# Conditioning units of 1024 columns, and a head's mean directly behind the split

## The chip, the cores and the metric

The kernel runs on one core of a Trainium2 chip. The metric is the time of one execution on the device in microseconds (us); lower is better. The names of the engines are those of the profile: PE is the matrix engine, DVE the vector engine, ACT the scalar engine, SP the engine that only issues transfers; GpSimd does nothing here.

## The reference

One sequence of 256 positions with 2048 features goes through two blocks, all in float32. Each sublayer is a norm, a modulation by vectors that come from a condition, a mixer, and a gated addition to `x`:

```
mod = silu(c) @ w_ada + b_ada              # 2048 -> 6*2048: sh1 sc1 ga1 sh2 sc2 ga2
h = rms_norm(x, g_norm1) * (1 + sc1) + sh1
qa, ka, va, oa, gates, qb, kb, vb = split(h @ w_in)
h_a = mlstm_bidirectional(qa, ka, va, gates)   # 4 heads of 256
h_a = h_a * rsqrt(mean(h_a**2) + eps) * g_head * sigmoid(oa)
h_b = neighborhood_attention(qb, kb, vb)       # 8 heads of 128
x = x + ga1 * (concat(h_a, h_b) @ w_out)
h = rms_norm(x, g_norm2) * (1 + sc2) + sh2
x = x + ga2 * conv_glu(h, w_up, w_down)
x = rms_norm(x, g_final)
# second block: the same frame twice, shift, scale, gate = silu(c2) @ ada_w + ada_b,
# once with a spatial gating unit (sgu), once with latent attention (mla)
```

The twelve modulation vectors need a product of one row with a matrix of 2048 x 24576: 201 MB of weights that are read for a single row.

## The kernel before

**Matrices.** Every large weight comes in pieces of 1 MB (the `w_down` pieces are smaller) through four slots `raw`. For each piece ACT writes the high part `w_hi`, rounded to float32r (`split`, L1105), DVE the low part `w_lo = raw - w_hi` over the slot of `raw` (`split`, L1557), and PE multiplies high by high, high by low and low by high (L575 and L576 for stages in columns, L614 to L616 for stages in tokens). The pieces have one order for the whole kernel (`STAGES`): `ka qa va qb kb vb oa` (together `w_in`, 8 pieces each), `w_out`, `w_up0`, `w_down0`, `w_up1`, `w_down1`, the `sgu` stages, `lat`, `mla_z`, `mla_v`, `heads`, `mla_out`. ACT and DVE are two pieces ahead of PE (`AHEAD`); SP issues the load of piece q when PE has done piece q - 4, and ACT may split piece q when PE has done piece q - 3 (there are three `w_hi`).

**Order on an engine.** Every engine runs its own list in order. For each piece ("slot") DVE first does `begin`: the split of the piece two ahead, then a possible urgent step, then the conditioning pieces that are put on this slot. After that it adds the second half of the product (`second_half`, L1611) and does what the slot has of attention. ACT's `begin` is the split and then the loads of conditioning pieces, each of which waits until DVE has used the buffer; then follow squares or exponents, the copy of the first half (L1124), roots.

**Conditioning.** The shift and scale of the first norm (the first 64 of 384 pieces of 512 KB) are made at the start by DVE and PE together (`first_piece`, L1622, on 128x1024). The other 320 pieces are DVE's alone (`add_ada`): a unit is 512 output columns, and a piece holds two of the 16 chunks of 128 input features for them. DVE adds each chunk, times silu(c), to `acc` (128x512): the second add waits for the first, `chain.link`. The last piece of a unit has an end: a transpose in 32x32 blocks (L1576) and a sum over 32 (L1577) to `fold`, from which PE makes the columns of `mods` with a few small matmuls (`fold_group`). `ADA_SPANS` says on which slots the pieces stand: (stage, first slot, slots, pieces), spread evenly. Four buffers `ada` hold them; ACT loads the piece four further on as soon as one is used.

**Heads of the mLSTM.** `A_STEPS` puts the steps of head k on slots: scores, mix, norm. After the mix DVE has `hf` (L1762, L1765); on the next slot (`A_SQUARES`: `qb` 2, `qb` 7, `kb` 4, `vb` 1) ACT takes the squares (L1202), DVE the mean (`a_head_mean`, L1771), ACT the root (L1207); on the slot behind it DVE starts with `a_head_diagonal` (L1775, L1777), PE multiplies by that diagonal after its own piece (L790), and DVE takes the result (L1783). Behind the heads come ten waves of neighbourhood attention, one per slot from `vb` 3 (`B_WAVES`): PE scores (L824), DVE arguments and maximum (L1805 to L1809), ACT exponents (L1230), on the next slot DVE's scaling as its urgent step (`b_scale`, L1792, L1794), PE transposes (L802), and so on. At the end of `w_in` the mixers' outputs are gated and split (`mix_high`, `gated` L1814, `mix_low` L1818) while PE begins `w_out`.

Of the kernel before, what the change touches and what calls it, by code (L numbers as in the profile page):

```python
# [76 lines left out]
for _name in STAGES:  # L77
# [6 lines left out]
    else:  # L84
# [8 lines left out]
SH1, SC1, GA1, SH2, SC2, GA2, S0, C0, G0, S1, C1, G1 = range(12)  # L93
UNITS = 4
UCOLS = D // UNITS
APIECES = 8
APIECE = D // P // APIECES * UCOLS
FIRST_UNITS = 2 * UNITS
QUARTERS = 4
FIRST_PIECES = QUARTERS * KC  # L100
K_PE = [3, 6, 9, 12]
# [3 lines left out]
FIRST_USED = QUARTERS * len(K_DVE)  # L105
ADA_SPANS = [("ka", 5, 11, 18), ("va", 0, 8, 15), ("qb", 0, 16, 28), ("vb", 0, 15, 19), ("w_out", 0, 13, 16),
             ("w_up0", 0, 40, 32), ("w_down0", 0, 32, 24), ("w_up1", 0, 44, 24), ("w_down1", 0, 26, 16), ("sgu_v", 3, 29, 40),
             ("sgu_u", 0, 32, 24), ("sgu_z", 0, 32, 24), ("sgu_out", 0, 28, 24), ("lat", 0, 20, 16)]
ADA_AT, _p = {}, FIRST_UNITS * APIECES
for _s, _j, _slots, _n in ADA_SPANS:  # L110
# [54 lines left out]
def build(nc, a):  # L165

    with ExitStack() as ctx:
# [49 lines left out]
        e1 = work("e1", [P, ASLOTS, APIECE], 0)  # L217
        acc_first = work("acc_first", [P, 2, 2 * UCOLS], 13312)
        row = work("row", [P, 2 * UCOLS], 15360)
        gw_lo = work("gw_lo", [P, GPAD], 4096, F32R)  # L220
# [16 lines left out]
        decay = work("decay", [P, 2, 2 * T], 13312)  # L237
        neg_rows = work("neg_rows", [P, 2 * T], 14336)
        bias_b = work("bias_b", [P, NH_B * 6, GRID_W], 14848)
        diag_a = at_("diag_a", [P, TT, P], o_nt)  # L240
# [32 lines left out]
        diag = work("diag", [P, TT, P], 2560)  # L273
        cst = work("cst", [P, 1152], 16384)
        turn, mask_m, cos, sin = cst[:, 0:256], cst[:, 256:640], cst[0:ROPE, 0:256], cst[0:ROPE, 640:896]
        rot, twice = cst[0:ROPE, 896:1024], cst[0:ROPE, 1024:1152]
        kr1 = work("kr1", [P, T], 13312)[0:ROPE, :]
        kro = work("kro", [P, T], 12288)
# [259 lines left out]
        def _(pe):  # L538
            def fold_group(n):


                v, count = FOLDS[n]
                if n == 0:
                    pe.wait_ge(sel_in, 16)
                    pe.wait_ge(unit_taken, FIRST_UNITS)
# [77 lines left out]
            def row_piece(q, k):  # L623

                p = q * KC + k
                if k == K_PE[0] and q:
                    pe.wait_ge(row_copied, 2 * q)
                pe.wait_ge(ada_full[p % 8], (p // 8 + 1) * 16)
                for v in range(2):
                    mm = pe.matmul(px[1 + v][0:1, :], csil[:, 0, k:k + 1], first_buf(p)[:, v * UCOLS:(v + 1) * UCOLS],  # L630
                                   start=(k == K_PE[0]), stop=(k == K_PE[-1]))
                mm.then_inc(ada_rowed, 1)
# [198 lines left out]
            def w_in_after(part, j):  # L831
                if (part, j) == ("ka", 7):
                    pe.wait_ge(rows_ready, 1)
                    for sc in range(TT):
                        pe.transpose(px[1][:, sc * GROW:(sc + 1) * GROW], gates[0:GROW, 5, sc * P:(sc + 1) * P],
                                     ident[0:GROW, 0:GROW])
                        mm = pe.transpose(px[1][:, (TT + sc) * GROW:(TT + sc + 1) * GROW], neg_rows[0:GROW, T + sc * P:T + (sc + 1) * P],
                                          ident[0:GROW, 0:GROW])
# [257 lines left out]
        def _(act):  # L1096
# [141 lines left out]
            for part, j in W_IN_PIECES:  # L1238
# [308 lines left out]
        def _(dve):  # L1547
# [166 lines left out]
            def gate_step(n):  # L1714
# [14 lines left out]
                elif n == 2:  # L1729
# [91 lines left out]
            for part, j in W_IN_PIECES:  # L1821
# [236 lines left out]
            for c in range(MH):  # L2058
# [90 lines left out]
def constants():  # L2149
# [53 lines left out]
def lay_out(i):  # L2203
# [107 lines left out]
```

## Time and profile before

| | |
|---|---|
| median of 3 runs | 2464.03 us (2463.12, 2464.03, 2468.52) |
| the profiled execution's own time | 2468.54 us |
| its span, first to last instruction | 2466.4 us |
| mean granted PE clock | 0.986 |
| busy: PE, DVE, ACT | 97%, 79%, 45% |
| instructions | 31962 |

Busy time is the time in which at least one instruction of the engine runs; PE's matmuls overlap, so its 97% does not say that it runs at its peak. A wait is named by the engine and instruction that ended it. The granted clock is PE's, as a share of 2.4 GHz.

### The profile page before, as it was taken

The page shows a single profiled execution, that of the slowest core. Times are in us where ns is not written, and L with a number is a line of the kernel's source. Part 1 is how long each engine was busy: PE and PEld are TensorE (multiplying, and loading weights), DVE is VectorE, ACT ScalarE, POOL GpSimd, SP SyncE. Part 2 cuts the span into 40 slices and gives each one's busy share as a digit, 9 for nine tenths or more (in the row PEclk, how much of TensorE's full clock was granted, in tenths as well). Part 3 has the DMA queues.
Part 4 walks back from the last instruction along what each step waited for, and adds up shares of the span by engine and source line. Part 5 has one row for each costly group of instructions (what it writes and reads, how often), then busy time and mean ns, then how long its engine had stood idle before and what let it go on. Part 6 is the DMA issues. An engine that isn't in the chain of part 4 may idle for free.

```text
span 2466.4 us, 31962 instructions
## 1 busy us (share of the span) xinstructions
PE 2402.6 (97%) x12970; PEld 2043.8 (83%) x12970; DVE 1947.9 (79%) x2412; ACT 1112.8 (45%) x1381; POOL 0.2 (0%) x4
## 2 busy tenths in 40 slices
PE   6999999998999999999998999999999998999999
PEld 3587888887888888888887888888888887888987
DVE  6789988898888788877787889778787666774754
ACT  2143444545444434444444444644445334555642
POOL 0000000000000000000000000000000000000000
PEclk8799999999999999999999999999999999999999
DMA  9799777585767688666685899766777774654343
GB/s 396 291 363 343 271 259 258 210 309 195 258 252 258 230 294 296 239 236 238 225 269 186 307 327 320 261 237 223 256 265 254 273 265 164 248 205 158 118 169 137
DMA packets 119011, 620.33 MB, mean 252 GB/s; under 512 B 13392, under 2 KB 14672, under 8 KB 76112
## 3 DMA queue, kind: packets, MB, share of 16 engines
q1 hardware_dynamic: 70560, 446.45, 51.1%
q10 hardware_dynamic: 48304, 171.82, 18.9%
q8 instruction: 103, 1.69, 0.3%
q14 instruction: 44, 0.36, 0.0%
HBM read 616.13 MB, written 2.10 MB: 251 GB/s over the span
## 4 chain that ended last, share of the span: by engine, by line
PE 77%; DVE 16%; DMA 3%; ACT 3%; issue 1%; ACTq 0%; SPq 0%; DVEq 0%
PE pm L575 21%; PE pm L576 11%; PE ps L575 10%; DVE w_lo L1557 7%; PE ps L576 5%; DVE acc L1570 5%; PE pm L614 5%; PE pm L616 5%; PE pm L615 5%; ACT w_hi L1105 2%; PE ps L614 2%; PE ps L616 2%; PE ps L615 2%; DMA ada<-in_ada 2%; PE px L894 1%
## 5 line engine op out<-in xcount | busy, mean ns | idle before, releaser
L1557 DVE TENSOR_TENSOR w_lo<-raw,w_hi 128x2048 fp32r<-128x2048 f32 (+2 forms) x412 | 891.8, 2165 | 312.7 <-ACT w_hi L1105 311.0
L1105 ACT ACTIVATE w_hi<-raw 128x2048 fp32r<-128x2048 f32 (+2 forms) x412 | 746.8, 1813 | 465.9 <-DMA raw<-in_w_down 124.9
L575 PE MATMUL pm<-h,w_hi 128*128 128x512 f32 x2318 | 826.3, 400 | 3.5 <-DVE w_lo L1557 3.0
L576 PE MATMUL pm<-h,w_lo 128*128 128x256 f32 x2318 | 651.0, 281 | 0.0
L575 PEld LDWEIGHTS pm<-h,w_hi 128*128 128x128 f32 x2318 | 436.4, 188 | 113.1 <-issue 7.6
L1570 DVE SCALAR_TENSOR_TENSOR acc<-ada,csil,acc 128x512 f32<-128x512 f32 x600 | 449.4, 749 | 12.7
L576 PEld LDWEIGHTS pm<-h,w_lo 128*128 128x128 f32 x2318 | 438.6, 189 | 0.2
L575 PE MATMUL ps<-h,w_hi 128*128 128x512 f32 x1186 | 422.9, 399 | 0.8 <-DVE w_lo L1557 0.8
L576 PE MATMUL ps<-h,w_lo 128*128 128x256 f32 x1186 | 332.8, 281 | 0.0
L575 PEld LDWEIGHTS ps<-h,w_hi 128*128 128x128 f32 x1186 | 222.7, 188 | 56.6 <-issue 2.7
L576 PEld LDWEIGHTS ps<-h,w_lo 128*128 128x128 f32 x1186 | 224.0, 189 | 0.1
L575 PE MATMUL pm<-glu,w_hi 128*128 128x512 f32 x484 | 170.0, 395 | 0.0
L614 PE MATMUL pm<-w_hi,h 128*128 128x512 f32 x352 | 139.0, 395 | 5.5 <-DVE h L1676 5.0
L615 PE MATMUL pm<-w_lo,h 128*128 128x512 f32 x352 | 137.8, 392 | 0.0
L616 PE MATMUL pm<-w_hi,h 128*128 128x512 f32 x352 | 137.8, 391 | 0.0
L576 PE MATMUL pm<-glu,w_lo 128*128 128x256 f32 x484 | 135.9, 281 | 0.0
L575 PEld LDWEIGHTS pm<-glu,w_hi 128*128 128x128 f32 x484 | 90.9, 188 | 21.4
L576 PEld LDWEIGHTS pm<-glu,w_lo 128*128 128x128 f32 x484 | 91.1, 188 | 0.0
L1342 ACT ACTIVATE conv<-conv 128x256 f32<-128x256 f32 x44 | 18.4, 418 | 157.9 <-DVE conv L1898 157.9
L614 PEld LDWEIGHTS pm<-w_hi,h 128*128 128x128 f32 x352 | 66.6, 189 | 19.9 <-issue 5.4
L616 PEld LDWEIGHTS pm<-w_hi,h 128*128 128x128 f32 x352 | 66.6, 189 | 14.1
L615 PEld LDWEIGHTS pm<-w_lo,h 128*128 128x128 f32 x352 | 66.7, 189 | 13.6
(430 smaller groups left out, 3034.8 us busy)
## 6 DMA issues: line engine op xcount, KB each, us to landing
ada<-in_ada ACTq DMA_DIRECT2D x320, 512.0 KB, 5.3
raw<-in_w_up SPq DMA_DIRECT2D x88, 1024.0 KB, 4.9
raw<-in_w_in SPq DMA_DIRECT2D x56, 1024.0 KB, 6.0
raw<-in_w_down SPq DMA_DIRECT2D x64, 704.0 KB, 5.2
raw<-in_sgu_v SPq DMA_DIRECT2D x32, 1024.0 KB, 5.1
raw<-in_sgu_u SPq DMA_DIRECT2D x32, 1024.0 KB, 5.0
raw<-in_sgu_z SPq DMA_DIRECT2D x32, 1024.0 KB, 4.9
raw<-in_sgu_out SPq DMA_DIRECT2D x32, 1024.0 KB, 5.0
```

What stands on the lines that cost most here:

```text
L575: pe.matmul(dst[:, :], wh[:, k, :], hl, start=(kc == 0), stop=False, skip_group_check=True)
L576: mm = pe.matmul(dst[:, 0:T], wl[:, k, :], hi, start=False, stop=last, skip_group_check=True)
L614: pe.matmul(dst[:, :], h_hi, wh[:, k, :], start=(kc == 0), stop=False, skip_group_check=True)
L615: pe.matmul(dst[:, :], h_hi, wl[:, k, :], start=False, stop=False, skip_group_check=True)
L616: mm = pe.matmul(dst[:, :], h_lo, wh[:, k, :], start=False, stop=(kc == 4 * parts - 1), skip_group_check=True)
L894: mm = pe.matmul(px[g % 4][:, c * T + n * P:c * T + (n + 1) * P], v_sgu[:, n, g * 2 * P + c * P:g * 2 * P + (c + 1) * P], mixw[s][:, r, 0: ...
L1105: act.activation(w_hi[:, q % HSLOTS, 0:n], raw[:, q % SLOTS, 0:n], ACT.Copy).then_inc(hi_ready, 1)
L1342: act.activation(conv[:, k % 2, :], conv[:, k % 2, :], ACT.Gelu).then_inc(gelu_ready, 1)
L1557: tt_(w_lo[:, q % SLOTS, 0:n], raw[:, q % SLOTS, 0:n], whole(w_hi[:, q % HSLOTS, 0:n]), ALU.subtract).then_inc(lo_ready, 1)
L1570: ins = stt(dst, w, c, dst, ALU.mult, ALU.add)
```

## The change

The change has two parts that speak of time and some moves of buffers.

- `UNITS` 4 becomes 2 and `APIECES` 8 becomes 16: a unit is 1024 columns, a piece (still 128 partitions of 1024 elements, 512 KB) holds one chunk of 128 input features for them. `add_ada` does one operation on 128x1024 per piece instead of two on 128x512; transpose and sum at the end of a unit are over 128x1024. There are still 320 pieces behind the start; the start itself keeps its widths (`QCOLS` takes the place of `UCOLS` there).
- `ADA_SPANS`: `ka` from slot 4 (17 pieces over 12 slots; before 18 over 11 from slot 5), `va` 13 (15), `qb` and `kb` 27 (28), `vb` and `oa` 20 over 14 slots (19 over 15), `w_out` 19 (16). From `w_up0` on nothing moves.
- `a_head_mean` becomes the urgent step of `begin` on its slots: behind the split, ahead of the conditioning pieces and of `second_half`, where it stood at the end of the slot.
- `acc` grows by 2 KB per partition. Room for it comes from: the second half of `neg_rows` goes to `gates[:, 7]`, the first into `nt`; `bias_b` moves by 512 columns; `cst` loses 128 columns, for which the doubled rotary key is read from partitions 64 to 127.

```diff
-UNITS = 4
+UNITS = 2
 UCOLS = D // UNITS
-APIECES = 8
+APIECES = 16
...
+QCOLS = D // QUARTERS
...
-ADA_SPANS = [("ka", 5, 11, 18), ("va", 0, 8, 15), ("qb", 0, 16, 28), ("vb", 0, 15, 19), ("w_out", 0, 13, 16),
+ADA_SPANS = [("ka", 4, 12, 17), ("va", 0, 8, 13), ("qb", 0, 16, 27), ("vb", 0, 14, 20), ("w_out", 0, 13, 19),
...
-FOLD_UNITS = 12
+FOLD_UNITS = 6
...
-        neg_rows = work("neg_rows", [P, 2 * T], 14336)
-        bias_b = work("bias_b", [P, NH_B * 6, GRID_W], 14848)
+        neg_rows = at_("neg_rows", [P, T], o_nt + T)
+        bias_b = work("bias_b", [P, NH_B * 6, GRID_W], 14336)
...
-        cst = work("cst", [P, 1152], 16384)
+        cst = work("cst", [P, 1024], 16384)
...
                 dve.wait_ge(ada_full[p % ASLOTS], p // ASLOTS * 16 + 16 - FIRST_PIECES // 8 * 16)
-                for r in range(2):
-                    w, c = ada[:, p % ASLOTS, r * UCOLS:(r + 1) * UCOLS], csil[:, cond, 2 * k + r:2 * k + r + 1]
-                    if k + r == 0:
-                        ins = ts_(dst, w, c, None, ALU.mult)
-                    else:
-                        ins = stt(dst, w, c, dst, ALU.mult, ALU.add)
-                    if r == 0:
-                        chain.link(ins)
+                w, c = ada[:, p % ASLOTS, :], csil[:, cond, k:k + 1]
+                if k == 0:
+                    ins = ts_(dst, w, c, None, ALU.mult)
+                else:
+                    ins = stt(dst, w, c, dst, ALU.mult, ALU.add)
                 if k == APIECES - 1:
                     chain.link(ins)
-                    turned = ada[:, p % ASLOTS, 0:UCOLS]
+                    turned = ada[:, p % ASLOTS, :]
...
-                    stt(neg_rows[G, T:2 * T], gates[G, 4, :], -1.0, gates[G, 6, :], ALU.mult, ALU.subtract).then_inc(rows_ready, 1)
+                    stt(gates[G, 7, :], gates[G, 4, :], -1.0, gates[G, 6, :], ALU.mult, ALU.subtract).then_inc(rows_ready, 1)
...
-                begin(part, j, (lambda: b_scale(w - 1)) if 0 < w <= NH_B else None, part != "ka" or j >= 2)
+                urgent = (lambda: b_scale(w - 1)) if 0 < w <= NH_B else None
+                if (part, j) in A_SQUARES:
+                    urgent = lambda: a_head_mean(A_SQUARES[part, j])
+                begin(part, j, urgent, part != "ka" or j >= 2)
...
-                if (part, j) in A_SQUARES:
-                    a_head_mean(A_SQUARES[part, j])
...
-                    tt_(kr1, kr1, krt, ALU.add).then_inc(kr_ready, 1)
+                    tt_(kr_sum, kr1, krt, ALU.add).then_inc(kr_ready, 1)
```

## Rows read from the trace of the kernel before

**Rows 1.** Busy time, share of the span and instructions of each engine
```profile
PE 2402.6 (97%) x12970; PEld 2043.8 (83%) x12970; DVE 1947.9 (79%) x2412; ACT 1112.8 (45%) x1381; POOL 0.2 (0%) x4
```
**Rows 2.** PE's waits: 120:250, 250:400, 400:470, 470:500, 600:835 (us, times, longest)
```profile
PE pm L575 <- DVE w_lo L1557: 2.3, 2, 1.7
PE pm L614 <- ACT va L1271: 0.5, 1, 0.5
...
PE px L790 <- DVE diag_a L1777: 4.1, 2, 3.1
...
PE px L802 <- DVE s_b L1794: 1.0, 1, 1.0
...
PE pm L575 <- DVE h L1818: 2.2, 1, 2.2
...
PE ps L575 <- DVE w_lo L1557: 0.8, 2, 0.6
PE pm L575 <- DVE w_lo L1557: 0.7, 3, 0.3
```
**Rows 3.** Stretches: us, busy of each engine, PE clock, DMA share, GB/s
```profile
349.80:353.20 3.40, 3.40 (x14) 3.11 (x15) 2.51 (x2) 2.93 (x3) 0.00 (x0) 0.51 0.91 337
...
483.00:486.40 3.40, 3.33 (x10) 2.84 (x11) 3.35 (x7) 3.40 (x5) 0.00 (x0) 0.50 0.17 72
```
**Rows 4.** SP's issues: first start, us to the last one's end, count
```profile
128.63 16.97 SPq L515 DMA_DIRECT2D raw<-in_w_in  x4
...
600.25 212.05 SPq L515 DMA_DIRECT2D raw<-in_w_up  x38
...
963.16 220.81 SPq L515 DMA_DIRECT2D raw<-in_w_up  x40
...
843.11 80.41 SPq L515 DMA_DIRECT2D raw<-in_w_down  x22
...
1210.13 89.73 SPq L515 DMA_DIRECT2D raw<-in_w_down  x24
```
**Rows 5.** DVE's groups, whole span: count, busy us, mean ns, idle before
```profile
L1570 DVE SCALAR_TENSOR_TENSOR acc<-ada,csil,acc 128x512 f32<-128x512 f32 x600 | 449.4, 749 | 12.7
L1622 DVE SCALAR_TENSOR_TENSOR acc_first<-e,csil,acc_first 128x1024 f32<-128x1024 f32 x24 | 30.8, 1284 | 7.3 <-DMA e<-in_ada 5.3 <-DVE acc_first L1622 0.5
L1576 DVE STREAM_TRANSPOSE ada<-acc 128x512 f32<-128x512 f32 x40 | 28.5, 712 | 1.4
L1577 DVE TENSOR_REDUCE fold<-ada 128x16 f32<-128x512 f32 x40 | 27.4, 686 | 1.4
```
**Rows 6.** Timeline of DVE and ACT at head 2: start, us, instruction, idle before
```profile
348.89 0.17 DVE L1775 RECIPROCAL small_a<-small_a 128x2 f32<-128x2 f32 x1 [0.27 <-ACT small_a L1207]
...
350.69 2.29 DVE L1557 TENSOR_TENSOR w_lo<-raw,w_hi 128x2048 fp32r<-128x2048 f32 x1 [1.12 <-ACT w_hi L1105]
...
341.43 0.42 ACT L1202 ACTIVATE sqt<-hf 128x256 f32<-128x256 f32 x1 [4.29 <-DVE hf L1765]
...
348.65 0.20 ACT L1207 ACTIVATE small_a<-small_a 128x2 f32<-128x2 f32 x1 [4.75 <-DVE small_a L1771]
```
**Rows 7.** Timeline of DVE: bias in `qa` 4, half of `oa` 6
```profile
187.24 3.36 DVE L1833 TENSOR_TENSOR bias_b<-bias_b,wmask 128x3072 f32<-128x3072 f32 x1
...
475.85 0.42 DVE L1611 TENSOR_TENSOR oa<-oa,pm 128x256 f32<-128x256 f32 x1
```
**Rows 8.** Timeline of DVE and PE at `vb` 5
```profile
406.00 0.62 DVE L1794 TENSOR_SCALAR s_b<-s_b,small_b 128x256 f32<-128x256 f32 x2
...
407.20 0.60 PE L802 MATMUL px<-ident,s_b 128*128 128x128 f32 x4
```
**Rows 9.** ACT's issues near 130 us, and the bias load's time to landing
```profile
130.04 0.46 ACTq L1251 DMA_DIRECT2D bias_b<-in_bias_b  x1
145.71 0.82 ACTq L1110 DMA_DIRECT2D ada<-in_ada  x2
...
bias_b<-in_bias_b ACTq DMA_DIRECT2D x1, 1536.0 KB, 15.6
```

More of the change, by code:

```diff
@@ L93 @@
 SH1, SC1, GA1, SH2, SC2, GA2, S0, C0, G0, S1, C1, G1 = range(12)
-UNITS = 4
+UNITS = 2
 UCOLS = D // UNITS
-APIECES = 8
+APIECES = 16
 APIECE = D // P // APIECES * UCOLS
-FIRST_UNITS = 2 * UNITS
 QUARTERS = 4
+QCOLS = D // QUARTERS
 FIRST_PIECES = QUARTERS * KC
@@ L105 @@
 FIRST_USED = QUARTERS * len(K_DVE)
-ADA_SPANS = [("ka", 5, 11, 18), ("va", 0, 8, 15), ("qb", 0, 16, 28), ("vb", 0, 15, 19), ("w_out", 0, 13, 16),
+ADA_SPANS = [("ka", 4, 12, 17), ("va", 0, 8, 13), ("qb", 0, 16, 27), ("vb", 0, 14, 20), ("w_out", 0, 13, 19),
              ("w_up0", 0, 40, 32), ("w_down0", 0, 32, 24), ("w_up1", 0, 44, 24), ("w_down1", 0, 26, 16), ("sgu_v", 3, 29, 40),
              ("sgu_u", 0, 32, 24), ("sgu_z", 0, 32, 24), ("sgu_out", 0, 28, 24), ("lat", 0, 20, 16)]
-ADA_AT, _p = {}, FIRST_UNITS * APIECES
+ADA_AT, _p = {}, FIRST_PIECES
 for _s, _j, _slots, _n in ADA_SPANS:
@@ L217, in build @@
         e1 = work("e1", [P, ASLOTS, APIECE], 0)
-        acc_first = work("acc_first", [P, 2, 2 * UCOLS], 13312)
-        row = work("row", [P, 2 * UCOLS], 15360)
+        acc_first = work("acc_first", [P, 2, 2 * QCOLS], 13312)
+        row = work("row", [P, 2 * QCOLS], 15360)
         gw_lo = work("gw_lo", [P, GPAD], 4096, F32R)
@@ L273, in build @@
         diag = work("diag", [P, TT, P], 2560)
-        cst = work("cst", [P, 1152], 16384)
+        cst = work("cst", [P, 1024], 16384)
         turn, mask_m, cos, sin = cst[:, 0:256], cst[:, 256:640], cst[0:ROPE, 0:256], cst[0:ROPE, 640:896]
-        rot, twice = cst[0:ROPE, 896:1024], cst[0:ROPE, 1024:1152]
-        kr1 = work("kr1", [P, T], 13312)[0:ROPE, :]
+        rot, twice = cst[0:ROPE, 896:1024], cst[ROPE:P, 896:1024]
+        kr_both = work("kr_both", [P, T], 13312)
+        kr1, kr_sum = kr_both[0:ROPE, :], kr_both[ROPE:P, :]
         kro = work("kro", [P, T], 12288)
@@ L544, in fold_group @@
                     pe.wait_ge(sel_in, 16)
-                    pe.wait_ge(unit_taken, FIRST_UNITS)
+                    pe.wait_ge(unit_taken, 2 * QUARTERS)
                 else:
@@ L629, in row_piece @@
                 for v in range(2):
-                    mm = pe.matmul(px[1 + v][0:1, :], csil[:, 0, k:k + 1], first_buf(p)[:, v * UCOLS:(v + 1) * UCOLS],
+                    mm = pe.matmul(px[1 + v][0:1, :], csil[:, 0, k:k + 1], first_buf(p)[:, v * QCOLS:(v + 1) * QCOLS],
                                    start=(k == K_PE[0]), stop=(k == K_PE[-1]))
@@ L836, in w_in_after @@
                                      ident[0:GROW, 0:GROW])
-                        mm = pe.transpose(px[1][:, (TT + sc) * GROW:(TT + sc + 1) * GROW], neg_rows[0:GROW, T + sc * P:T + (sc + 1) * P],
+                        mm = pe.transpose(px[1][:, (TT + sc) * GROW:(TT + sc + 1) * GROW], gates[0:GROW, 7, sc * P:(sc + 1) * P],
                                           ident[0:GROW, 0:GROW])
@@ L971, in doubled_key @@
                 pe.wait_ge(kr_ready, 1)
-                pe.matmul(px[1][:, T:2 * T], twice, kr1, start=True, stop=True).then_inc(kr_twice, 1)
+                pe.matmul(px[1][:, T:2 * T], twice, kr_sum, start=True, stop=True).then_inc(kr_twice, 1)
             for c in range(MH):
@@ L1165, in copy_rows @@
                 for v in (1, 0):
-                    act.activation(row[0:1, v * UCOLS:(v + 1) * UCOLS], px[1 + v][0:1, :], ACT.Copy).then_inc(row_copied, 1)
+                    act.activation(row[0:1, v * QCOLS:(v + 1) * QCOLS], px[1 + v][0:1, :], ACT.Copy).then_inc(row_copied, 1)
             def first_chunks(q):
@@ L1246, in _ @@
                     for k in range(ASLOTS):
-                        load_ada(FIRST_UNITS * APIECES + k)
+                        load_ada(FIRST_PIECES + k)
                 if (part, j) == ("ka", 4):
                     act.dma_start(wmask[:, :], a["wmask"]).then_inc(wmask_in, 16)
-                    act.wait_ge(unit_summed, FIRST_UNITS)
+                    act.wait_ge(unit_summed, 2 * QUARTERS)
                     act.dma_start(flat(bias_b[:, :, :]), a["bias_b"]).then_inc(bias_in, 16)
@@ L2162, in constants @@
     win = np.where((c[None] >= lo) & (c[None] < lo + WIN_COLS), 0.0, NEG).astype(f)
-    cst = np.zeros((P, 1152), f)
+    cst = np.zeros((P, 1024), f)
     half = ROPE // 2
@@ L2177, in constants @@
     for m in range(P):
-        cst[m % ROPE, 1024 + m] = 1.0
+        cst[ROPE + m % ROPE, 896 + m] = 1.0
     sel = np.zeros((P, 2 * P - BLOCK), f)
@@ L2268, in lay_out @@
     ada = np.concatenate([i["w_ada"][0], i["ada_w_2"][0], i["ada_w_2"][1]], axis=1)
-    first = ada[:, 0:2 * D].reshape(KC, P, 2, QUARTERS, UCOLS).transpose(3, 0, 1, 2, 4).reshape(-1, P, APIECE)
+    first = ada[:, 0:2 * D].reshape(KC, P, 2, QUARTERS, QCOLS).transpose(3, 0, 1, 2, 4).reshape(-1, P, APIECE)
     ada = ada.reshape(APIECES, KC // APIECES, P, 12 * UNITS, UCOLS).transpose(3, 0, 2, 1, 4)
```

## The prediction

> **What bounds the kernel now.** The page comes first: TensorE (PE) is busy 97% of the span [rows 1], so whatever VectorE (DVE) saves counts only where PE waits for DVE. The waits of PE say where that is [rows 2]. Behind the start, which the change leaves alone, and outside the norms, whose waits hang on squares, sums and roots that no conditioning piece stands ahead of, they are: 2.3 us on `w_lo` and 0.5 us on the copy of `va` between 120 and 250 us; 4.1 us on `diag_a` (heads 0 and 2, the longest 3.1) between 250 and 400; 1.0 us on `s_b`; 2.2 us on `h` at the end of `w_in`; and 0.8 + 0.7 us on `w_lo` in `w_up0`. That is 11.6 us. Two of them cost more than they last: behind the 3.1 us wait and behind the 2.2 us wait the granted clock is 0.51 and 0.50 for 3.4 us (the 1.2 GHz level) [rows 3], 1.7 us of PE's work each, while the 1.7 us wait among those on `w_lo` is followed by no such row.
>
> The third view is the queue of weight loads, because one `raw` load is issued as each piece ends on PE. In `w_up0` 38 issues start over 212 us, (212.05 - 0.33) / 37 = 5.72 us a piece; in `w_up1`, the same matmuls, 40 over 220.8, 5.65 us [rows 4]. So `w_up0` loses 37 x 0.07 = 2.6 us, more than its 1.5 us of visible waits. But PE has also two paces of its own: four issues in `ka` stand 5.55 us apart, and those in `w_up1`, where no wait on DVE is seen, 5.65 [rows 4]. I return to that below. From `w_up1` on PE waits for DVE nowhere except at the norms and once each for a residual and a head.
>
> **The change part by part.** (1) *Piece adds.* 320 pieces behind the first norm. Now a piece is two adds of 128x512, 0.749 us each; then it is one of 128x1024, and that very form stands in the start: 1.284 us [rows 5]. Per piece 2 x 0.749 - 1.284 = 0.21 us, and a step between dependent adds of 0.03 us less: 0.25 us. The first piece of a unit is a plain multiply, cheaper in both; it changes the sum little.
> (2) *Unit ends.* 40 become 20. One costs 0.712 + 0.686 us now [rows 5]. For twice the columns the bounds are 1.40 us (nothing saved) and half of the fixed part less; with the slope of the adds, (1.284 - 0.749) / 512 = 1.04 ns a column, it is 1.24 + 1.22 = 2.46 us. I take 2.5. Sum over the kernel: 300 x 0.25 + 20 x (2.8 - 2.5) + first pieces, some 85 us of DVE time; nearly all of it lies where PE is at its own pace and buys nothing.
> The Trainium skill ("VectorE: DVE Perf Modes", the section on the TRN2 errata) says that operations on SBUF pay a fixed latency once per instruction, and gives (N + 151) / 0.96 ns for a float32 add. By that a merged pair would save 0.16 us instead of 0.21; the row decides, and either frees more than the waits need.
>
> (3) *Slots.* Counting the spans out: through `qa` 7 DVE has 6.5 us less of this work, through `va` 7 15 us, through `kb` 4 22 us. The ends of units fall on `qa` 6, `qb` 0, `kb` 2, `vb` 4 and `w_out` 1 instead of `qa` 1, `qa` 6, `va` 2, `va` 6, `qb` 3, `kb` 0, `kb` 4, `vb` 1, `vb` 7 and `oa` 6. Each new one is a lump: piece and end are 3.8 us, now 2.9.
>
> (4) *The mean.* Today it stands behind the adds and the second half. At head 2 ACT's root waits for it until 348.65, 4.75 us idle, and ACT takes up its next split only then, so that DVE stands 0.27 us before the reciprocal and 1.12 us before `w_lo` [rows 6]. Directly behind the split DVE finds ACT's squares done (two of 0.42 us [rows 6] under a split of 2.3 us, so the wait on `a_sq` is covered; uncovered it would be about 1.2 us for each of four heads, with the adds behind it). The root, the next split and `diag_a` no longer wait for the adds: 0.16 + 0.27 + 1.12, about 1.5 us of DVE time per head.
>
> (5) `neg_rows`, `kr_sum` and `cst` change places, not sizes (cst is 64 KB smaller, its load is hidden): nothing.
>
> Now the waits, one after another.
> *120 to 250 us:* the `w_lo` wait of 1.7 us follows the 3.4 us bias addition in `qa` 4 [rows 7]. The 6 us less of adds before it cover the 1.7. The `va` copy waits in ACT behind loads that wait for DVE's adds; that goes too. Gain 2.8 to 3.0 us; I take 3.0.
> *Head 0 and head 2:* from the point where DVE waits for PE's scores of head 2 in `kb` 1 I add up: split 2.3, adds 4.6 (`kb` 2, now 3.1), half 0.4, split 2.3, adds 2.6 (`kb` 3, now 1.5), half 0.4, then the mix at about 337, 2 us ahead of today; `kb` 4 has one piece (1.3) where two and an end stand today (4.5 us). `diag_a` is there at about 344.4, and PE asks for it at 346.6. Gain 4.1 us and the slow stretch of 1.7: 5.8 (bounds 1.0, head 0 alone, and 5.8).
> *`s_b`:* `vb` 7 has 2.0 us less ahead of it: 1.0 us.
> *End of `w_in`:* `oa` 6 loses its piece and unit end, 2.9 us, but its half cannot be added before PE and ACT deliver it, near 474.4 against 475.85 [rows 7]; from there the chain of `hx`, gate and `h` is as long as before. So only some 1.1 us of the first wait go, and 0.4 us come back at the next four chunks: 0.7 us. The rest is too short for a slow stretch, by the 1.7 us wait that had none: 1.7 more. Gain 2.4 (bounds 0.7 and 3.9).
> *`w_up0`:* the loop split, adds, `glu`, half, split, adds, taps, gelu, split paces it; per ten pieces the adds fall from 13.9 to 10.3 or 12.4 us, enough for PE's pace: 2.6 us (bounds 1.5 and 2.6).
> *A new wait:* `vb` 4 gets 4.6 us of adds where it has 1.5. Behind them stand the arguments of wave 1, ACT's exponents, and after the next split the scaling, at 406.00, for which PE asks at 407.20 [rows 8]. DVE reaches `vb` 4 about 1 us earlier; it is through 3.1 - 1.0 = 2.1 us later than now, and the scaling, 0.62 us and the reciprocal's step, ends at 408.8 to 409.0 against 407.2: a loss of 1.8 us (bounds 0 and 3.5, the latter with a slow stretch).
> *The start at `ka` 4:* two ACT loads are issued near 140 instead of 145.71 us [rows 9], while the raw load for `qa` 0 is under way; `w_lo` has under 1 us to spare there. Bounds 0 and 2 us. The bias load, issued at 130.04, is in flight for 15.6 us [rows 9] on the same ACT queue, up to about 146, so the new loads stand behind it: I take 0.
> The Trainium skill ("DMA: Bandwidth & Descriptors", Queues, rings and completion order) says that each DMA engine takes turns between the queue rows that have work, packet by packet. By that, SP's load keeps its turn as long as ACT's row has work anyway, which it has here; it speaks against the early start only where ACT's queue is empty.
>
> **Sum:** 3.0 + 5.8 + 1.0 + 2.4 + 2.6 - 1.8 - 0 = 13.0 us. The profiled execution took 2468.5 us (span 2466.4), so its like would take 2455.5. The median of the runs is 2464.0, 4.5 us less. The two paces explain such a step (44 pieces of `w_up1` x 0.1 = 4.4), though no row shows it. I carry the 13.0 over: **2451.0 us**.
>
> **Rivals.** *Part of it only* (2459): the heads and the end of `w_in` are held by PE and ACT, not by DVE; then 3.0 + 1.0 + 2.6 - 1.8 = 4.8 us go. For it: the head's chain has six hand-overs. Against: DVE is idle under 0.5 us at a time there, except for the 1.12. *The lumps bite more* (2455): the `vb` 4 wait brings a slow stretch, and another comes at `qb` 0 or `kb` 2. *Early loads* (2453, or 2455 with a slow stretch): the loads pulled to 140 us take bandwidth from the raw load, and PE waits up to 2 us for `qa` 0. *Pace, upward:* pieces at 5.65 us fall to 5.55; of `w_up1` alone 4.4 us, 2446; all 160 such pieces 16 us, 2435. *Pace, downward, the slower case:* PE's own pace turns from fast to slow in stretches that this change does not touch, since the end of a wait sets it anew. `w_down0` stands at 3.81 us and `w_down1` at 3.89 [rows 4]: 32 x 0.07 = 2.4 us; `w_up1` of the median run 4.4. The kernel becomes slower than before by 0.2% only from 18 us on, 1.9% of some 950 us of matmuls that now run fast. No row speaks for so many at once.
>
> **Numbers.** The forecast with all its terms 0.60 (its own range 2446 to 2456); part only 0.14; lumps 0.08; early loads 0.03; pace upward 0.09; pace downward 0.06, of which 0.03 ends slower. Range 2443 to 2460: up to the partial case above, and to `w_up1` and one more stage at the fast pace below. Within 0.2%, 4.9 us, a measurement can't tell from no change: faster means below 2459.1. Partial cases split there, so faster 0.84, same 0.12, slower 0.04.
>
> **What would show it.** Adds of 128x1024 at 1.28 us, 300 of them, unit ends near 2.5 us; no wait on `diag_a`, or one under 0.5 us; no `w_lo` wait between 150 and 250; a wait of 1 to 2 us on `s_b` near 400 us, in another wave than now; one of 1 to 1.5 us at the start of `w_out`, no stretch of 0.5 clock from 120 us to the second norm; `w_up0` at 5.65 us a piece; every stage from `w_down0` on as long as before but for steps of 0.1 us per piece. Wrong would be: `diag_a` still waited for (ACT is late, not DVE), `w_lo` waits in `w_up0` at the unit ends (`w_up0` 18 and 38), or a new wait at `qa` 0.

## The result and the profile after

The changed kernel takes 2452.38 us (median of 5 runs, 2449.22 to 2455.29); the kernel before, on the same chip, 2465.75 (5 runs, 2463.12 to 2468.52). The ratio is 0.9944 with an interval of 0.9933 to 0.9955: 13.4 us or 0.56% faster. The forecast was 2451.0 (2443 to 2460), 13.0 us less than a median of 2464.0. The profiled execution took 2449.22 us, its span is 2447.3 us, the mean granted clock 0.990.

The page's row of busy time, which answers to [rows 1]:

```profile
PE 2390.6 (98%) x12970; PEld 2037.4 (83%) x12970; DVE 1873.4 (77%) x2052; ACT 1115.4 (46%) x1381; POOL 0.2 (0%) x4
```

DVE is busy 74.5 us less, and the time fell by a fifth of that: DVE did not bound the kernel, it only made PE wait in places. The groups of DVE that answer to [rows 5]:

```profile
L1570 DVE SCALAR_TENSOR_TENSOR acc<-ada,csil,acc 128x1024 f32<-128x1024 f32 x300 | 383.9, 1280 | 1.5
L1574 DVE STREAM_TRANSPOSE ada<-acc 128x1024 f32<-128x1024 f32 x20 | 24.9, 1245 | 0.7
L1575 DVE TENSOR_REDUCE fold<-ada 128x32 f32<-128x1024 f32 x20 | 24.4, 1220 | 0.7
L1568 DVE TENSOR_SCALAR acc<-ada,csil 128x1024 f32<-128x1024 f32 x20 | 15.0, 748 | 0.1
```

An add of 128x1024 takes 1.280 us, as the start's form did. A unit end is 2.47 us (1.245 + 1.220) where 2.5 was reckoned. The last number of a row, idle time before the group, fell from 12.7 to 1.5 us for the adds: the waits between the two dependent halves are gone.

PE's waits, in the same stretches as [rows 2] (the work stands 7 to 17 us earlier). Between 120 and 250 us there is none. Between 250 and 400, and between 400 and 470, one each:

```profile
PE px L803 <- DVE s_b L1792: 1.7, 1, 1.7
...
PE pm L576 <- DVE h L1816: 0.8, 1, 0.8
```

Of the 11.6 us of waits the 0.8 on `h` are left, and 0.3 on `w_lo` at the beginning of `w_up0`. The 1.7 us on `s_b` are new: they stand in another wave than the 1.0 did. The granted clock of the whole stretch, which holds no half-clock part as [rows 3] had (columns as there):

```profile
120.00:560.00 440.00, 434.21 (x2359) 373.18 (x2358) 382.61 (x408) 204.91 (x235) 0.00 (x0) 1.00 0.81 291
```

The new wait comes from what stands in DVE's timeline around `vb` 4 (start, us, instruction):

```profile
382.07 0.62 DVE L1792 TENSOR_SCALAR s_b<-s_b,small_b 128x256 f32<-128x256 f32 x2
382.60 1.28 DVE L1570 SCALAR_TENSOR_TENSOR acc<-ada,csil,acc 128x1024 f32<-128x1024 f32 x1
383.91 1.25 DVE L1574 STREAM_TRANSPOSE ada<-acc 128x1024 f32<-128x1024 f32 x1
385.19 1.22 DVE L1575 TENSOR_REDUCE fold<-ada 128x32 f32<-128x1024 f32 x1
386.44 0.75 DVE L1568 TENSOR_SCALAR acc<-ada,csil 128x1024 f32<-128x1024 f32 x1
387.23 0.76 DVE L1803 SCALAR_TENSOR_TENSOR s_b<-px,bias_b 128x256 f32<-128x256 f32 x2
...
391.22 0.62 DVE L1792 TENSOR_SCALAR s_b<-s_b,small_b 128x256 f32<-128x256 f32 x2
```

The end of the unit and the first piece of the next, 4.6 us together, stand ahead of the arguments of the wave (387.23), so its scaling is done at 391.8, and PE's transposes start then, 1.7 us late.

**Stage by stage.** For each piece the trace has the moment at which PE reports it done, and the table takes differences of those (us). "start" runs to the end of `ka` 3 (the first half of `ka`), which the change does not touch; "rest" is everything behind `w_up1` up to the last piece of `mla_out`. All kernels that ran stand in it, since the executions of one kernel lie 5 to 18 us apart. A single stage repeats within a few tenths where nothing waits and the pace is the same; the two traces of the kernel before differ by some 1.5 us in `qb`, `kb` and in `vb`, by 2.7 in `w_down0` and by 4.6 in `w_up1`.

| kernel | start | ka | qa, va | qb, kb | vb | oa | w_out | w_up0 | w_down0 | w_up1 | rest | without start |
|---|---|---|---|---|---|---|---|---|---|---|---|---|
| before | 128.6 | 22.2 | 93.2 | 122.6 | 53.9 | 59.0 | 93.4 | 261.7 | 122.9 | 248.7 | 1247.1 | 2324.8 |
| e11 before again | 124.0 | 22.5 | 93.1 | 121.1 | 55.5 | 59.0 | 93.6 | 262.3 | 125.6 | 244.1 | 1244.6 | 2321.4 |
| after | 121.9 | 22.6 | 88.5 | 116.5 | 55.7 | 57.8 | 90.9 | 260.0 | 123.5 | 248.9 | 1248.0 | 2312.4 |
| e8 after again | 121.4 | 22.7 | 88.5 | 116.5 | 55.7 | 57.6 | 91.0 | 260.0 | 122.9 | 248.7 | 1246.8 | 2310.5 |
| e1 mean back | 121.4 | 22.2 | 89.4 | 116.5 | 55.7 | 57.7 | 91.0 | 259.5 | 122.9 | 248.7 | 1249.6 | 2313.2 |
| e2 mean only | 125.3 | 22.6 | 92.5 | 117.6 | 53.8 | 59.0 | 93.5 | 261.8 | 125.3 | 244.1 | 1247.0 | 2317.2 |
| e3 old spans | 121.5 | 23.2 | 89.4 | 116.5 | 53.8 | 57.8 | 94.1 | 259.9 | 123.2 | 244.4 | 1248.1 | 2310.4 |
| e4 two halves | 121.4 | 23.9 | 88.5 | 116.5 | 55.9 | 57.7 | 91.0 | 259.9 | 123.2 | 248.7 | 1247.3 | 2312.7 |
| e9 halves waited | 128.3 | 22.6 | 89.2 | 117.0 | 57.9 | 57.8 | 92.9 | 261.1 | 122.9 | 248.7 | 1249.3 | 2319.3 |
| e5 spans only | 123.8 | 22.3 | 90.5 | 117.2 | 57.9 | 58.8 | 92.2 | 261.9 | 122.9 | 248.7 | 1245.4 | 2317.7 |
| e6 end moved | 125.4 | 22.2 | 89.4 | 116.5 | 53.8 | 58.7 | 90.9 | 260.4 | 124.0 | 248.7 | 1249.8 | 2314.3 |
| e10 end alone | 121.6 | 22.2 | 89.3 | 116.5 | 53.8 | 57.7 | 91.0 | 260.6 | 124.1 | 248.7 | 1250.6 | 2314.4 |
| e12 adds alone | 121.6 | 22.6 | 88.5 | 116.5 | 53.8 | 57.7 | 95.5 | 260.4 | 123.4 | 248.7 | 1248.5 | 2315.6 |
| e7 start ka 5 | 122.0 | 23.4 | 88.5 | 116.5 | 55.7 | 57.8 | 91.0 | 259.5 | 122.9 | 248.7 | 1250.3 | 2314.3 |

### The profile page after: what moved, and what is told of

Its sections match the earlier page's. It is cut to its first block, busy times and chain, and to the rows that moved or that the text cites. A ratio compares the mean times of both kernels' runs of the same rounds, so it can differ in the third digit from the quotient of the medians.

```text
span 2447.3 us, 31602 instructions
## 1 busy us (share of the span) xinstructions
PE 2390.6 (98%) x12970; PEld 2037.4 (83%) x12970; DVE 1873.4 (77%) x2052; ACT 1115.4 (46%) x1381; POOL 0.2 (0%) x4
## 4 chain that ended last, share of the span: by engine, by line
PE 80%; DVE 2%; ACT 0%; DMA 0%; issue 0%; ACTq 0%; DVEq 0%
PE pm L576 24%; PE pm L577 12%; PE ps L576 12%; PE ps L577 6%; PE pm L615 4%; PE pm L616 4%; PE pm L617 4%; PE ps L615 2%; PE ps L616 2%; PE ps L617 2%; DVE w_lo L1558 1%; PE px L895 1%; PE pm L594 0%; DVE x L2023 0%; PE ps L594 0%; PE pm L1011 0%
## 5 line engine op out<-in xcount | busy, mean ns | idle before, releaser
L1570 DVE SCALAR_TENSOR_TENSOR acc<-ada,csil,acc 128x1024 f32<-128x1024 f32 x300 | 383.9, 1280 | 1.5
L576 PEld LDWEIGHTS pm<-glu,w_hi 128*128 128x128 f32 x484 | 90.9, 188 | 21.9 <-DVE w_lo L1558 0.4
```

Source lines behind the costliest of these rows:

```text
L576: pe.matmul(dst[:, :], wh[:, k, :], hl, start=(kc == 0), stop=False, skip_group_check=True)
```

## The experiments

The change has three parts that speak of time: the wide units with their merged adds, the new slots, and the early mean. The moves of buffers stand in every variant of the changed kernel, e9 included, and were not tested by themselves. Sums "without the start" are the last column of the table.

### Is it the mean? (e1, e2)

e1 is the changed kernel with the mean back at the end of the slot; e2 is the kernel before with only the mean moved.

```diff
-                urgent = (lambda: b_scale(w - 1)) if 0 < w <= NH_B else None
-                if (part, j) in A_SQUARES:
-                    urgent = lambda: a_head_mean(A_SQUARES[part, j])
-                begin(part, j, urgent, part != "ka" or j >= 2)
+                begin(part, j, (lambda: b_scale(w - 1)) if 0 < w <= NH_B else None, part != "ka" or j >= 2)
...
+                if (part, j) in A_SQUARES:
+                    a_head_mean(A_SQUARES[part, j])
```

> The changed kernel with the mean of a head put back behind the second half of its slot. If the wide adds carry the gain (my theory), DVE reaches the head steps early anyway: the wait on diag_a stays under 0.5 us at every head, each head shows again the idle 1.1 us before w_lo, and the time is that of the changed kernel within 2 us (2451 to 2454). If the moved mean carries the 5.8 us of heads 0 and 2 (rival), a wait of 2 to 3 us on diag_a comes back with a stretch at half the clock, and the time is 2456 to 2458.

> The kernel before with the mean behind the split and nothing else. My theory: diag_a at head 2 comes 1 to 2 us earlier and the 3.1 us wait shrinks to 1.5 to 2 us without the slow stretch, the waits on w_lo, s_b and h at the end of w_in stay; 2459 to 2463. Rival (the mean is the change): all head waits go, 2457. Rival (the mean is nothing): 2465.

e1: 2450.09 us (2446.92 to 2457.46), ratio 0.9952 (0.9936 to 0.9968): as fast as the change. Its `qb` and `kb` take the same 116.5 us, and its waits up to the end of `w_in` are those of the changed kernel. e2: 2457.72 us (2455.01 to 2467.27), 0.9979 (0.9965 to 0.9994), so the mean alone gives some 5 us. I had expected 2459 to 2463; the rival's 2457 is what came, though not all head waits went, as it said. PE's waits of e2 between 120 and 400 us:

```profile
PE pm L575 <- DVE w_lo L1557: 2.0, 2, 1.7
PE px L790 <- DVE diag_a L1777: 0.7, 1, 0.7
PE pm L614 <- ACT va L1271: 0.4, 1, 0.4
PE ps L614 <- DVE qa L1611: 0.2, 1, 0.2
```

The wait on `diag_a` at head 2, 3.1 us before, is gone, where I had expected half of it to stay, and 0.7 of 1.1 us stay at head 0. The waits on `w_lo` (2.0 us, 2.3 before), `va`, `s_b` and `h` are within 0.3 us of [rows 2]. The mean alone cures head 2, and beside the other parts it is worth nothing: that wait was cured more than once.

### Is it the slots? (e3, e5, e7)

e3 is the changed kernel with the old `ADA_SPANS`, e5 the kernel before with the new ones, e7 the changed kernel with `("ka", 5, 11, 17)`, which undoes the early start alone.

```diff
-ADA_SPANS = [("ka", 4, 12, 17), ("va", 0, 8, 13), ("qb", 0, 16, 27), ("vb", 0, 14, 20), ("w_out", 0, 13, 19),
+ADA_SPANS = [("ka", 5, 11, 18), ("va", 0, 8, 15), ("qb", 0, 16, 28), ("vb", 0, 15, 19), ("w_out", 0, 13, 16),
```

> Wide units and the moved mean, but the pieces on the slots of before (18, 15, 28, 19, 16). Ends of units then fall on qa 6, va 6, kb 0, vb 1 and oa 6. My theory: the wait of 1.7 us on s_b at vb 5 goes, since the lump is not on vb 4, and the wait on h at the start of w_out grows from 0.8 to 2 us or more, perhaps with 3.4 us at half the clock, since oa 6 has a piece and an end again; in all within 2 us of the changed kernel. Rival (the spread is what gains): 2457 or more.

> The kernel before, units of 512 columns and the mean where it was, with only the new slots for the pieces (17, 13, 27, 20, 19). My theory: one to two pieces fewer before the waits in qa and va and at head 2, and none on oa 6: 1 to 4 us faster than before, 2461 to 2464. Rival (the spread is the gain): 2455 or less.

> The changed kernel with the first conditioning piece on ka 5 as before (17 pieces over 11 slots). My theory (the early loads stand behind the bias load): within 1 us of the changed kernel. Rival (early loads take bandwidth from the raw load of qa 0): the piece of qa 0 or the one before is 0.2 to 2 us shorter than in the changed kernel.

e3: 2452.93 us (2444.97 to 2457.92), ratio 0.9949 (0.9931 to 0.9966). In the table it has 53.8 us in `vb` and 94.1 in `w_out`. The new spans lose 1.9 us in `vb` by their lump and give 3.2 in `w_out`, so 1.3 us net, which the medians here can't tell. What `w_out` had is a wait on `h` as before the change, and slow clock behind it (waits from 460 to 480 us, and a stretch of 3.4 us):

```profile
PE pm L576 <- DVE h L1816: 2.8, 1, 2.8
```
```profile
467.60:471.00 3.40, 3.40 (x13) 2.87 (x13) 3.24 (x7) 2.53 (x3) 0.00 (x0) 0.56 0.00 0
```

e5: 2460.09 us (2454.23 to 2466.91), ratio 0.9996 (0.9982 to 1.0011). Without the cheaper adds the gain of the slots alone can't be told from nothing by the times; the one trace is 3.7 to 7.1 us shorter without the start than the two of the kernel before. It shows them give and take: the wait on `diag_a` falls from 4.1 to 0.2 us, and `s_b` is waited for 4.4 us in three waves, one of them 1.9, which was not expected.

e7: 2450.96 us (2444.30 to 2456.01), ratio 0.9960 (0.9945 to 0.9975). `ka` took 23.4 us against 22.6, `qa` 0 6.12 us in both: the early loads cost nothing, as forecast. The tenths that `ka` varies by (22.2 to 23.9) go with neither start slot.

### Is it the width of the operation? (e4, e9)

Both keep units, ends, slots and mean of the change, and add each piece as two operations on the halves of the unit. In e4 the two don't wait for each other; in e9 the second waits for the first (the two lines marked with +9), so that the adds cost what they cost before.

```diff
-                w, c = ada[:, p % ASLOTS, :], csil[:, cond, k:k + 1]
-                if k == 0:
-                    ins = ts_(dst, w, c, None, ALU.mult)
-                else:
-                    ins = stt(dst, w, c, dst, ALU.mult, ALU.add)
+                c = csil[:, cond, k:k + 1]
+                for r in range(2):
+                    cols = slice(512 * r, 512 * (r + 1))
+                    w, part = ada[:, p % ASLOTS, cols], acc[:, cols]
+                    if k == 0:
+                        ins = ts_(part, w, c, None, ALU.mult)
+                    else:
+                        ins = stt(part, w, c, part, ALU.mult, ALU.add)
+9                    if r == 0:
+9                        chain.link(ins)
```

> The changed kernel, each piece added in two operations of 128x512 on the halves of its 1024 columns, with no wait between them: units, ends, slots and mean are those of the changed kernel, only the merged operation is gone. My theory (DVE's time per piece is what counts): adds cost 1.50 us a piece again, waits on w_lo in qa and in w_up0 and one on diag_a come back, 2459 to 2465. Rival (unit width, slots and mean do it): 2451 to 2453.

> The changed kernel with each piece added as two operations on 128x512 (the halves of the unit) and the second made to wait for the first, so that a piece costs DVE what it did before the change (about 1.53 us against 1.28 with one operation and 1.41 with two that don't wait, as the previous run showed), while slots, mean and unit ends stay those of the change. If DVE time per piece is what the change lives on: the rows between the third piece of ka and the end go back toward the kernel before with the new spans alone: w_lo waits in w_up0 return (w_up0 261.5 to 262 us against 260.0), w_out near 92 against 91, vb 57 to 58 against 55.7 with two s_b waits, about 5 to 6 us longer in all than the changed kernel; kb and qb stay cured by the early mean and the slots. If it is the width of a unit and the place of its ends: all stages as in the changed kernel within 1 us.

e4: 2449.46 us (2445.75 to 2454.21), ratio 0.9940 (0.9919 to 0.9961), as fast as the change. Up to `w_up1` its stages are within 0.3 us of the change's, except `ka` (1.3 longer). My expectation of 2459 to 2465 was wrong: the merged operation as such does not carry the gain, and a piece did not cost the 1.50 us that I had put down. The groups of DVE show why, first of e4, then of e9:

```profile
L1573 DVE SCALAR_TENSOR_TENSOR acc<-ada,csil,acc 128x512 f32<-128x512 f32 x600 | 422.8, 746 | 1.5
```
```profile
L1573 DVE SCALAR_TENSOR_TENSOR acc<-ada,csil,acc 128x512 f32<-128x512 f32 x600 | 449.7, 749 | 12.1
```

600 operations of 746 ns would be 447.6 us one behind the other, and the group is busy 422.8: the two of a piece overlap. With the idle time a piece costs 1.41 us in e4, 1.54 in e9 ((449.7 + 12.1) / 300), 1.28 in the change. Half of the saving is that the operations of a piece no longer depend on each other, half that there is one instead of two.

The Trainium skill ("VectorE: DVE Perf Modes", the section on the TRN2 errata) says that the latency to SBUF is exposed between instructions and that one large tile pays it once. This case agrees in kind: one add in place of two free ones saves 1.41 - 1.28 = 0.13 us, where its formula for the addition of two tensors (151 cycles at 0.96 GHz) gives 0.16. The further 0.13 us that a wait between them costs, measured here, are not in that formula.

e9: 2458.24 us (2456.07 to 2462.51), ratio 0.9978 (0.9969 to 0.9987). Against the change and its second trace, without the start, it is 6.9 to 8.8 us longer; the expectation for costly adds said 5 to 6. 1.7 us of this are a stretch at half clock that the change does not have. In `w_up0` it lost 1.1 us where 1.5 to 2 were expected. Its waits up to the end of `w_in`, and the clock behind the largest:

```profile
PE px L803 <- DVE s_b L1797: 2.2, 1, 2.2
PE pm L576 <- DVE h L1821: 0.8, 1, 0.8
PE pm L576 <- DVE ka L1614: 0.5, 1, 0.5
PE px L791 <- DVE diag_a L1780: 0.4, 1, 0.4
PE ps L615 <- DVE qa L1614: 0.3, 1, 0.3
```
```profile
400.50:403.90 3.40, 3.40 (x11) 2.71 (x9) 0.86 (x2) 2.05 (x3) 0.00 (x0) 0.50 0.76 239
```

`vb` is 57.9 us: 53.8 without the lump, 2.2 of wait and 1.7 of half clock make 57.7. So with the new slots and mean in place, DVE's time per piece is worth 7 to 9 of the 12 to 14 us. The first 0.13 us a piece give all of it: e4 takes 2312.7 us without the start, the change, with another 0.13 us less, 2312.4 and 2310.5.

### The adds alone (e12)

The changed kernel with the edits of e1 and of e3 together, so that only the wide units are left.

> The changed kernel with both the old spans and the mean back at the end of the slot, so that only the 1024 column units (one add of 1.28 us a piece, 20 ends of 2.5 us) are left of the change. Two runs have cured head 2 by the mean alone and by the spans alone; this one is to show whether the adds do it alone. If the adds carry nearly the whole gain and each of the three is enough for the heads: qb and kb 116.5 to 117.5 us, no wait on diag_a over 0.5 us, qa and va 88.5 to 89.5, vb 53.8, w_out 94.1 with the wait of 2.8 us on h (as with the old spans before), w_up0 259.5 to 260.0; without the start 2310 to 2313 us, median within 3 us of the changed kernel. If the heads need the mean or the slots beside the adds: qb and kb 118 to 121 us with 1 to 3 us of wait on diag_a, and 2313 to 2318 us without the start.

2451.90 us (2440.09 to 2457.89), ratio 0.9947 (0.9925 to 0.9970). The adds alone take the waits of both heads away, `qa` to `oa` take 316.5 us, less than in the changed kernel (318.5), so the change's other parts are of no use there. Up to the end of `w_in` one wait is left, and the clock behind it:

```profile
PE pm L576 <- DVE h L1816: 3.0, 1, 3.0
```
```profile
464.30:471.10 6.80, 6.00 (x19) 5.14 (x20) 6.63 (x11) 4.31 (x6) 0.00 (x0) 0.50 0.07 28
```

The granted clock is at half for 6.8 us, and `w_out` takes 95.5 us against 90.9. That is more than the 94.1 that I expected, and so is the sum without the start, 2315.6 us against 2310 to 2313. The adds carry the gain up to `oa`; the new spans give `w_out` its part.

Three runs have now taken away head 2's wait, each with one part of the change, but not equally well. How much DVE has to spare there is read from when it writes `diag_a` and when PE begins to use it, in e2 (mean alone), e12 (adds alone) and the changed kernel:

```profile
342.03 0.48 DVE L1777 TENSOR_SCALAR diag_a<-ident,small_a 128x128 f32<-128x128 f32 x2
342.57 1.16 PE L790 MATMUL px<-diag_a,hf 128*128 128x128 f32 x8
```
```profile
330.98 0.48 DVE L1775 TENSOR_SCALAR diag_a<-ident,small_a 128x128 f32<-128x128 f32 x2
333.97 1.05 PE L791 MATMUL px<-diag_a,hf 128*128 128x128 f32 x8
```
```profile
330.95 0.48 DVE L1775 TENSOR_SCALAR diag_a<-ident,small_a 128x128 f32<-128x128 f32 x2
334.28 1.05 PE L791 MATMUL px<-diag_a,hf 128*128 128x128 f32 x8
```

With the mean alone `diag_a` is there 0.1 us before PE takes it (in e5, the slots alone, it is 0.1 too), with the adds alone 2.5 us, with all three 2.8.

### The new wait (e6, e10)

The change's unit end stands on `vb` 4. e6 moves it to `vb` 6 together with the first piece of the next unit, e10 moves it there alone:

```diff
-("vb", 0, 14, 20)
+("vb", 0, 5, 6), ("vb", 6, 1, 2), ("vb", 7, 7, 12)      # e6
+("vb", 0, 5, 6), ("vb", 6, 1, 1), ("vb", 7, 7, 13)      # e10
```

> The changed kernel with the pieces of vb and oa laid out so that the unit end of vb 4 falls on vb 6, which has no wave behind it (6 pieces on vb 0 to 4, 2 on vb 6, 12 on vb 7 to oa 5). My theory: the 1.7 us wait on s_b near 390 us goes, no other takes its place, and nothing else moves: 1.5 to 2 us under the changed kernel. Rival: the two pieces a slot in oa make the scaling of a later wave late, and PE waits there instead: no change.

> The changed kernel with the unit end of vb 4 put alone on vb 6, without the first piece of the next unit that stood beside it in the run with the end moved, where PE still waited 0.6 us for s_b and oa took 58.7 us instead of 57.8. If the loss is DVE being late by the work ahead of the scaling: without the 0.76 us of that multiply no s_b wait is left, vb 53.8 and oa 57.8 us, that is 1.9 us less than the changed kernel behind the third piece of ka (2310.5 or less). If the wave itself sets a floor: the wait stays at 0.5 us or more and oa at 58.7. The medians can't tell 1.9 us; the trace can.

e6: 2447.98 us (2444.89 to 2454.77), ratio 0.9942 (0.9921 to 0.9963). `vb` falls from 55.7 to 53.8 us, but PE waits in a later wave: 0.6 us on `s_b`, and `oa` rises by 0.9. What came lies between the two expectations. e10: 2449.19 us (2445.75 to 2450.77), ratio 0.9937 (0.9922 to 0.9952). DVE at the same place:

```profile
396.35 1.28 DVE L1570 SCALAR_TENSOR_TENSOR acc<-ada,csil,acc 128x1024 f32<-128x1024 f32 x1
397.67 1.25 DVE L1574 STREAM_TRANSPOSE ada<-acc 128x1024 f32<-128x1024 f32 x1
398.94 1.22 DVE L1575 TENSOR_REDUCE fold<-ada 128x32 f32<-128x1024 f32 x1
400.20 2.29 DVE L1558 TENSOR_TENSOR w_lo<-raw,w_hi 128x2048 fp32r<-128x2048 f32 x1
```

No wait on `s_b` is left, `vb` is 53.8 and `oa` 57.7: the 1.9 us are back, and the loss was DVE's lateness alone. The sum expected without the start, 2310.5 or less, did not come: it is 2314.4, since `w_down0` took 0.6 to 1.2 us and the rest 2.6 to 3.8 more than in the two traces of the change. These differ between executions of one kernel, and the intervals of e10 and the change overlap; that e10 is the faster kernel is shown for its two stages, not for its time.

### How much differs by itself (e8, e11)

e8 is the changed kernel, e11 the kernel before, both unaltered.

> The changed kernel unaltered, once more. The stages from ka 3 to the end should repeat within 1 us in sum; what differs between executions should lie in the first 115 us, where stretches at half the clock stand at other places, and be up to 6 us. If instead PE's two paces (5.55 and 5.65 us a piece) are drawn anew in each execution, w_up1 or the sgu stages differ by 3 to 4 us each.

> The kernel before, unaltered, for a second trace of it. If stages repeat and only the start and PE's pace differ between executions: qa to oa 328.7 us within 0.5, w_up0 261.8, while the first piece of ka ends anywhere between 110.9 and 118.1 us and w_up1 is 248.7 or 244.2. If the waits themselves differ from execution to execution: some of the waits on diag_a, w_lo or h are missing or of another size by over 0.5 us.

e8: 2452.79 us (2445.59 to 2458.58), ratio 0.9963 (0.9947 to 0.9979), so a second measurement gives 0.37% where the first gave 0.56. Its sum without the start is 1.9 us from the first trace's, where I expected at most 1, and `w_up1` kept its pace. e11: 2464.24 us (2459.00 to 2471.94), ratio 1.0002 (0.9989 to 1.0015). The profiled span of e11 is 2458.8, of before 2466.4. PE's waits of e11 between 250 and 400 us, and the stretches behind the head's, which ends at 345.4:

```profile
PE px L790 <- DVE diag_a L1777: 4.2, 2, 3.2
PE px L802 <- DVE s_b L1794: 1.5, 1, 1.5
```
```profile
345.00:348.40 3.40, 3.02 (x20) 2.77 (x21) 2.28 (x3) 3.40 (x3) 0.00 (x0) 1.00 0.96 355
348.40:351.80 3.40, 3.40 (x21) 3.01 (x20) 3.26 (x6) 0.09 (x1) 0.00 (x0) 1.00 0.56 187
```

The waits on `w_lo`, `diag_a` and `h` repeat within 0.2 us. Two things don't. The 3.2 us wait is followed by full clock here and was followed by half clock in [rows 3]; later, behind piece `vb` 4, PE waits 1.5 us for the `s_b` of the first wave, which it did not in the first trace, and `vb` takes 55.5. So the stretch at half clock cost nothing in the end: `qb` to `vb` take 176.5 us in the one trace and 176.6 in the other, because DVE is through with that `s_b` 53.7 and 53.9 us after the end of `kb` 5, and PE comes early for it or just in time. And PE's pace differs. The queue of weight loads (44 issues for `w_up1`, first start and length), of e11 and of the changed kernel:

```profile
945.14 233.88 SPq L515 DMA_DIRECT2D raw<-in_w_up  x44
```
```profile
925.76 238.25 SPq L516 DMA_DIRECT2D raw<-in_w_up  x44
```

4.4 us less for the same 44 pieces: 5.55 us each in place of 5.65.

## Why the prediction was right, point by point

*120 to 250 us*, 3.0 us of waits: right, all are gone. `qa` and `va` gained 4.7. By the pieces' ends the four waits had made their pieces 3.9 us longer, 0.1 to 0.3 more each than the wait itself lasts; the other 0.8 is `qa` running at 5.55 us a piece where it had 5.65. That pace is chance: in e1, e3, e6 and e10, which have the new adds too, `qa` stays at 5.65. `ka` lost 0.4.

*Heads 0 and 2*, 5.8 us with the slow stretch: 6.1 measured (122.6 to 116.5), and against e11 4.6. The wait is settled, and DVE was the cause as forecast: `diag_a` was to come 2.2 us before PE asks (344.4 and 346.6) and comes 2.8 before. Its slow stretch is not part of every execution, and booking 1.7 us for it was luck: in e11, without it, the same time was lost to the wait behind `vb` 4. With `vb` taken in, the change gains 4.3 us against the one trace and 4.4 against the other, where the forecast has 5.8 - 1.8 = 4.0. The step summed what needs no summing: the mean alone (e2), the slots alone (e5) and the adds alone (e12) each take head 2's wait away, the first two with 0.1 us to spare. Head 0 keeps 0.7 us with the mean alone and 0.4 in e9; with the adds alone nothing.

*`s_b`*, 1.0: right, `oa` gained 1.2.

*End of `w_in`*, 0.7 + 1.7: 2.5 measured, with another split: the wait fell by 1.4 (2.2 to 0.8, where 1.1 were to stay), so 1.1 are left for the slow stretch. e3 shows that it takes the spans: with the old ones the wait is 2.8.

*`w_up0`*, 2.6: mis-sized; 1.7 measured. I took the loss as 38 pieces at 5.72 against 5.65. By the pieces' ends 11 were longer than 5.67, by 3.5 us in all, but one of these is the stage's fifth piece, 6.49 us and still 6.23 in the changed kernel, and 10 ran at 5.55 and gave 1.0 us back. Afterwards that one and 39 pieces at 5.65 are left: 2.2 us, of which the first piece, behind the norm, took 0.35 back.

*The new wait at `vb` 5*, -1.8: right in place and size (1.7 us of wait, 1.8 in the stage; e6 and e10 give it back).

*Early loads*, 0: right (e7).

*Sum*: 13.0 forecast, 12.4 measured without the start (14.3 against the second trace of the change, 9.0 to 10.9 against e11). That it comes so near is in part luck: up to `w_up0` the change gains 13.9 us, and 1.5 are lost again from `w_down0` on, where the forecast had nothing; stages there differ by as much between two executions of one kernel.

*The 4.5 us between the profiled execution and the median*, put down to PE's two paces: the step exists but does not carry that (and with five runs in place of three they are 2.8 us). e11 has `w_up1` 4.6 us shorter, yet `w_down0` 2.7 longer, while its start is 4.6 us shorter. In the start the granted clock is at half for 41.6 us in before, 27.3 in e11 and in the trace of the change, 20.5 in e1, e3, e4, e8, e10 and e12; the first piece of `ka` ends at 118.1, 113.4, 111.4 and 110.9 to 111.1 us. I left this spread out of the range, and it did no harm because it is in the medians of both. In these traces the start is at half clock longer where the adds depend on each other (27.3 to 42.2 us in five, 20.5 to 37.5 in nine without), though none of those adds runs there. I take it for chance, because the medians don't follow it: e2, e5 and e9 lie 5.1, 7.5 and 5.6 us above the change (2452.6 as the mean of its two medians), and their sums without the start 4.8 to 8.8 above it. The granted clock over all executions speaks for chance too: measured on one chip, its mean is 0.9889 over 25 executions of the kernel before and 0.9886 over ten of the change (e8), while 14 us more at half clock would lower it by 0.003. PE's pace stays without a cause. In the stages listed piece by piece it changes only at a piece that is itself longer, and `w_up1` ran at 5.55 in e11, e2 and e3 alone.

The rivals: *part only* is refuted by the waits of the heads and of `h`; *lumps bite more* by the clock of 1.00 through 560 us; *pace, upward* and *downward* did not come in `w_up1` (5.65 us in both), though e3 shows the one in a kernel that has the new adds. e9, where 2.2 us of wait brought the half clock, shows that it was near.

## What to carry to other kernels

Where a vector engine feeds a bound matrix engine, count its savings only at the waits that it ends, and expect them to saturate: here 0.13 us a piece bought as much as 0.25, and each of three cures alone took away the same wait, two of them with 0.1 us to spare. A stretch at half clock behind a wait is worth counting only if nothing further on makes the engine wait for the same neighbour anyway. Before an operation is made wider for its fixed cost, see whether its parts depend on each other; taking the dependence away gave half. And where work is lumped anew, look which urgent step is next behind the lump: 4.6 us at the wrong slot cost 1.8 us; two slots later, and without the multiply of the next unit beside it (3.8 us), the lump cost nothing.

## What the runs showed that was not expected

- Two adds of 128x512 on DVE that don't depend on each other take 1.41 us together, two dependent ones 1.54, one of 128x1024 1.28.
- The same matmuls run at 5.55 or at 5.65 us a piece for a whole stage of 44, and that stage differs by 4.6 us between two executions of one kernel.
- A wait of about the same length is followed by 3.4 us at half clock or is not: 3.1 us yes and 3.2 no at head 2, 2.2 yes in e9 at `vb`, 1.9 no in e4, 1.7 no in the change. The 2.2 us wait on `h` was followed by it in all three traces that have it, and the 3.0 us of e12 by 6.8 us. So the cost of a wait is its length and, by chance, 1.7 us or more besides, and even these can be absorbed: in the kernel before they were, by DVE's lateness behind `vb` 4.
